# Part of a depthwise convolution handed from VectorE to GpSimd beside attention

## The reference

```python
def conv_group(a, b, conv_w, conv_b, g_ln, b_ln):
    h = a * jax.nn.sigmoid(b)                      # 512 channels
    h = lax.conv_general_dilated(h, conv_w[:, None, :].astype(h.dtype), window_strides=(1,),
                                 padding=[(CONV_K - 1, 0)], dimension_numbers=('NWC', 'WIO', 'NWC'),
                                 feature_group_count=CONV_CH) + conv_b      # CONV_K = 31 taps
    h = layernorm(h, g_ln, b_ln)
    return jax.nn.silu(h)
...
        conv_out = conv_group(z[..., :CONV_CH], z[..., CONV_CH:c0], ...)
        attn_out = mla_group(z[..., c0:c1], z[..., c1:c2], z[..., c2:], pos, ...)   # 8 causal heads
        mixed = jnp.concatenate([rmsnorm(attn_out, g_out_attn[l]), rmsnorm(conv_out, g_out_conv[l])], axis=-1)
        h = h + mixed @ w_out[l]
        h = h + peer_ffn(rmsnorm(h, g_ffn_norm[l]), ...)
```

## Time and profile before

| what | us |
|---|---|
| median of 3 runs | 2993.78 (2993.04 to 2997.05) |
| span of the profiled execution | 2989.1 |
| what lies around the span, as median less span | 4.7 |
| stage `mla` in the trace, first to last instruction | about 125.2 to 263.7 |
| TensorE busy over the span | 2885.6 (97%) |
| DVE, ACT, POOL busy over the span | 1787.5, 999.9, 1035.9 |

### The profile page before, as it was taken

How to read it: one execution, slowest core, us unless ns; L and a number is a source line. 1 busy time by engine, 2 the same in 40 slices (tenths; PEclk the granted TensorE clock), 3 DMA queues, 4 the chain that set the end, 5 groups by cost and what they waited for, 6 DMA issues and landing times. The chain is left out here.

```text
span 2989.1 us, 39368 instructions
## 1 busy us (share of the span) xinstructions
PE 2885.6 (97%) x14960; PEld 2560.3 (86%) x14960; DVE 1787.5 (60%) x3343; ACT 999.9 (33%) x1582; POOL 1035.9 (35%) x642
## 2 busy tenths in 40 slices
PE   8897999999999999999999999999999899899998
PEld 7655799999999999999998887888788788778886
DVE  6776778989888687888885834331043456333211
ACT  4355233444444222222223223222223466322222
POOL 3412400211213242333434444444432344444442
PEclk9997999999999999999999999999999699999999
DMA  3101247787969998999993322233331000222332
GB/s 129 39 1 54 88 146 224 251 271 224 298 205 350 320 330 300 324 325 325 326 325 113 106 85 88 96 99 104 94 133 38 4 1 15 82 95 94 96 102 67
DMA packets 195743, 475.82 MB, mean 159 GB/s; under 512 B 17204, under 2 KB 104116, under 8 KB 193252
## 3 DMA queue, kind: packets, MB, share of 16 engines
q1 hardware_dynamic: 114100, 343.27, 34.5%
q0 software_dynamic: 27648, 100.68, 9.7%
q10 hardware_dynamic: 53808, 29.36, 3.2%
HBM read 415.47 MB, written 56.62 MB: 158 GB/s over the span
## 5 line engine op out<-in xcount | busy, mean ns | idle before, releaser
L263 ACT ACTIVATE w_hi<-w 128x1024 fp32r<-128x1024 f32 (+2 forms) x485 | 506.4, 1046 | 1248.9 <-DVE ffn_gates L2156 324.4
L273 POOL TENSOR_TENSOR w_lo<-w,w_hi 128x1024 fp32r<-128x1024 f32 (+2 forms) x229 | 542.1, 2378 | 697.0 <-ACT w_hi L263 696.9
L273 DVE TENSOR_TENSOR w_lo<-w,w_hi 128x1024 fp32r<-128x1024 f32 x256 | 313.4, 1224 | 149.7 <-ACT w_hi L263 119.1
L308 PE MATMUL peer_psum<-xn_hi,w_hi 128*128 128x416 f32 x1024 | 365.9, 357 | 0.0
L1486 POOL DMA_INDIRECT peer_gathered<-in_peer_u,peer_chosen_here x96 | 152.3, 1586 | 614.0 <-DVEq L1741 483.4
L308 PE MATMUL peer_psum<-peer_w_hi,w_hi 128*128 128x416 f32 x1024 | 359.3, 351 | 3.2 <-DVE peer_w_lo L405 2.4
L309 PE MATMUL peer_psum<-xn_lo,w_hi 128*128 128x416 f32 x1024 | 360.9, 352 | 0.0
L310 PE MATMUL peer_psum<-xn_hi,w_lo 128*128 128x416 f32 x1024 | 360.7, 352 | 0.0
L309 PE MATMUL peer_psum<-peer_w_lo,w_hi 128*128 128x416 f32 x1024 | 358.0, 350 | 0.0
L310 PE MATMUL peer_psum<-peer_w_hi,w_lo 128*128 128x416 f32 x1024 | 358.0, 350 | 0.0
L308 PE MATMUL ffn_psum<-ffn_hn_hi,w_hi 128*128 128x512 f32 x704 | 276.0, 392 | 10.4 <-DVE ffn_hn_lo L618 6.6
(11 more groups left out here) (421 smaller groups left out, 5675.5 us busy)
## 6 DMA issues: line engine op xcount, KB each, us to landing
w<-in_peer_uT SPq DMA_DIRECT2D x128, 512.0 KB, 4.4
w<-in_peer_v SPq DMA_DIRECT2D x128, 512.0 KB, 5.5
w<-in_f_w_gu SPq DMA_DIRECT2D x88, 512.0 KB, 3.6
peer_act<-peer_act_out SPq DMA_DIRECT2D x128, 208.0 KB, 5.4
peer_gate<-peer_gates_out ACTq DMA_DIRECT2D x26, 1024.0 KB, 8.7
peer_gates<-peer_gate SPq DMA_DIRECT2D x16, 1664.0 KB, 9.5
peer_act_in<-peer_act SPq DMA_DIRECT2D x128, 208.0 KB, 4.6
w<-in_f_w_down SPq DMA_DIRECT2D x32, 512.0 KB, 3.5
```

The costliest lines, as they stand in the source:

```text
L263: act.activation(self.hi[:, x, 0:c], self.buf[:, x, 0:c], ACT.Copy).then_inc(self.rounded, 1)
L273: eng.tensor_tensor(self.lo[:, x, 0:c], self.buf[:, x, 0:c], self.hi[:, x, 0:c].bitcast(F32), ALU.subtract).then_inc(self.split, 1)
L308: pe.matmul(out, w[0], x[0], start=start, stop=False)
```

## The change

Three parts of the code change:

- In `front` the 25 taps go to tiles 0 and 1 alone (`POOL_TILE` = 2 caps `there`).
- In `mla` GpSimd makes taps 0 to 21 of tile 2 itself. Tap 0 is one `tensor_scalar` into the accumulator; each other tap is a `tensor_scalar` into one of two slots of a scratch tile (`scale_tap`) and a `tensor_tensor` that adds it to the accumulator (`add_tap`): 22 + 21 instructions of 128x512. They stand in GpSimd's queue between the 31 diagonals: 8 diagonals first, then per tap up to 4/3 further ones ahead of `scale_tap(k+1)` and `add_tap(k)`. The diagonals' `tensor_scalar` gets a second operation (times 1.0).
- VectorE has 93 - 25 - 22 = 46 taps left in `mla`, and `conv_steps` goes from 18 to 16, so `per_step` becomes 3 and all steps that hang on `first` stand two items earlier. A step takes taps of tiles 0 and 1 while there are any (37, so through n = 11 and one more at n = 12); then VectorE waits for all 22 taps of GpSimd (`tap_added`) and goes on with the 9 last taps of tile 2.

TensorE's own code is the same: two taps per item for n up to 15.

```diff
+POOL_TILE, POOL_TAPS = CT - 2, 22
...
-                        conv.run(dve, own, TAPS[key], there)
+                        conv.run(dve, own, TAPS[key], min(there, POOL_TILE))
...
-        conv_steps = 18
+        conv_steps = 16
+        assert conv.taps[on_tensor] == 0 and conv.taps[POOL_TILE] == 0
+        conv.taps[POOL_TILE] = POOL_TAPS
         per_step = -(-(CK * (CT - 1) - sum(conv.taps)) // conv_steps)
-        assert conv.taps[on_tensor] == 0
+        tap_scaled, tap_added = st.sem("tap_scaled"), st.sem("tap_added")
...
             @block.gpsimd
             def _(pool):
-                for k in range(CK):
-                    if k >= DIAGS:
-                        pool.wait_ge(diag_used, k - DIAGS + 1)
-                    pool.tensor_scalar(diag[:, k % DIAGS, :], kit.ident[:, :], kit.gain("conv_w", k * CT + on_tensor), None,
-                                       ALU.mult).then_inc(diag_made, 1)
+                def diagonals(k0, k1):
+                    for k in range(k0, k1):
+                        if k >= DIAGS:
+                            pool.wait_ge(diag_used, k - DIAGS + 1)
+                        pool.tensor_scalar(diag[:, k % DIAGS, :], kit.ident[:, :], kit.gain("conv_w", k * CT + on_tensor), 1.0,
+                                           ALU.mult, ALU.mult).then_inc(diag_made, 1)
+
+                def scale_tap(k):
+                    src = io["conv_in"][:, POOL_TILE, NMETA + k:NMETA + k + SEQ]
+                    w = kit.gain("conv_w", k * CT + POOL_TILE)
+                    if k == 0:
+                        pool.tensor_scalar(acc[:, POOL_TILE, :], src, w, kit.gain("conv_b", POOL_TILE), ALU.mult, ALU.add)\
+                            .then_inc(tap_added, 1)
+                        return
+                    if k >= 3:
+                        pool.wait_ge(tap_added, k - 1)
+                    pool.tensor_scalar(squared4[:, k % 2, :], src, w, 1.0, ALU.mult, ALU.mult).then_inc(tap_scaled, 1)
+
+                def add_tap(k):
+                    pool.wait_ge(tap_scaled, k)
+                    pool.wait_ge(tap_added, k)
+                    pool.tensor_tensor(acc[:, POOL_TILE, :], acc[:, POOL_TILE, :], squared4[:, k % 2, :], ALU.add)\
+                        .then_inc(tap_added, 1)
+
+                made = DIAGS
+                diagonals(0, made)
+                scale_tap(0)
+                scale_tap(1)
+                for k in range(1, POOL_TAPS):
+                    more = min(CK, DIAGS + k * 4 // 3)
+                    diagonals(made, more)
+                    made = more
+                    if k + 1 < POOL_TAPS:
+                        scale_tap(k + 1)
+                    add_tap(k)
+                diagonals(made, CK)
...
                 def between(n):
                     if n < conv_steps:
-                        conv.run(dve, taps, per_step)
+                        own_left = min(per_step, sum(CK - k for k in conv.taps[:POOL_TILE]))
+                        conv.run(dve, taps, own_left, POOL_TILE)
+                        if own_left < per_step and conv.taps[POOL_TILE] < CK:
+                            dve.wait_ge(tap_added, POOL_TAPS)
+                            conv.run(dve, taps, per_step - own_left)
```

## The result

The changed kernel takes 3013.02 us, median of 4 runs (3011.4 to 3013.88), beside 2993.41 us (2990.62 to 2997.05) for the kernel before on the same chip: a ratio of 1.0064 with an interval of 1.005 to 1.0079, slower. The profiled execution took 3012.59 us with a span of 3010.8, so what lies around the span is 1.8 us. For the kernel before it isn't the 4.7 of the prediction either: a further profiled execution of it took 2992.97 us for a span of 2991.0, 2.0 around it, so the execution whose span of 2989.1 the prediction started from was probably one of about 2991 us, quicker than the median.

The account below looks back on a forecast made before the run. TensorE was taken to bound the attention stage, VectorE's taps lying beside its work up to item 15. Terms +14.6 + 5.6 - 1.0 = +19 us on a span of 2989.1 give 3008, plus 4.7 makes 3013; range 2998 to 3025.

Parts of the forecast that it names:

- the 4.7 of the prediction: Around the profiled span: 4.7 us between span and median, added to the span of 3008 to give 3013.
- The new stall: At item 12 in mla, VectorE waits 17.5 us for GpSimd's last add, until 196.8 us, and TensorE's attention work stops.
- even without contention VectorE waits 12 us: At item 12: GpSimd alone is done at 185 us, while VectorE wants its result at 173.2.
- GpSimd's time: GpSimd's queue in mla: 22 scales, 21 adds and 31 diagonals take 58.3 us alone; with contention done at 196.8.
- +0.2 for a diagonal: GpSimd beside VectorE's taps: a diagonal grows by 0.2 us, a scale or an add by 0.45.
- VectorE's pace: VectorE before the wait: 1.15 us a tap beside GpSimd, 4.27 us an item, item 12's tap at 178.3 us.
- The sum for this part: Stage start to carry-over: item 16's carry-over at about 208.7 us against 194.10 for item 18's before, +14.6.
- The 1.5 us for TensorE's low clock: Behind the stall, ahead of the carry-over: TensorE returns with its clock down, which adds 1.5 us.
- second rival: VectorE and GpSimd exclude each other for whole instructions; TensorE also waits for diagonals past item 9: +31 us, 3025; chance 0.12.
- Light contention: GpSimd's long instructions disturb VectorE as little as diagonals do; GpSimd done at 185 us: +7 us, 3001; chance 0.13.
- Not slower: GpSimd is done before VectorE asks at 173.2 us, leaving only the gains of 1.5 and 1 us: 2991; chance 0.05.
- the mis-sized term: Behind the carry-over: two more items cost 5.6 us, and the norms' steps two items earlier give back 1.0.

Follow-up runs that it names:

- The first experiment: Changed kernel, but GpSimd sums its 22 taps in its own tile, joined by one add at the carry-over, so no wait at item 12: 3001.66 us, ratio 1.0041.
- the spare-work run: Kernel before, all 68 VectorE taps kept, with GpSimd doing the changed kernel's 22 taps and 31 diagonals into an unread spare tile: 3014.12 us, ratio 1.0081.
- the two versions with GpSimd's own sum: Changed kernel with GpSimd's 22 taps summed in its own tile and joined at the carry-over: conv_steps 16, 3001.66 us (1.0041); conv_steps 18, 2995.14 us (1.0013).

## Why the prediction was right, and where its terms were off

**The new stall: as said.** VectorE waits once, ahead of tap L667, for GpSimd's add, at item 12: 17.5 us forecast, 16.92 measured; adds at 1.26 us alone and 1.69 beside taps, nine taps behind the wait at 0.77 us (2.31/3), TensorE idle for 11.71 us, its clock at 0.59 behind it. The first experiment confirms the price: without that wait 10.5 of the 19.6 us are gone. What the wait is made of was not as said: "even without contention VectorE waits 12 us" failed, since with no taps beside GpSimd it waits 4.92, and contention makes the larger part of the 16.92.

**GpSimd's time: 3.5 us off, by two errors that partly cancel.** Alone it was put at 58.3 us; it takes 51.9. Adds (26.7 forecast, 26.5 measured) and scales (16.1; 14.5 + 0.8) were right; the diagonal was priced at 0.5 us and takes 0.367, so 4.4 us too much. The old form without the second operation took 0.587 at its quickest; the two-operation row was the better neighbour and still too high. Contention was put at 13 us (196.8 - 125.3 against 58.3) and is 16.2 (68.1 - 51.9), and nearly half of it is on the diagonals: 18.5 - 11.1 = 7.4 us, with 3.9 on the adds and 4.2 on the scales. The step "+0.2 for a diagonal", read off 0.73 against 0.587, failed: a diagonal beside taps goes from 0.36 to 0.80, +0.45 like the long instructions. The price of 0.587 without taps was not the error: in the trace of the kernel before a diagonal of 0.60 us stands at 147.78, between four taps that start at 144.87 and end at 147.60 and the next at 148.47. But the old diagonals overlapped taps only for part of their row, so the mean of 14, 0.73 us, hides what one loses beside a tap: the one at 148.64, beside a tap, took 1.04.

```profile
144.87 2.73 DVE L667 SCALAR_TENSOR_TENSOR mixT<-conv_in,gains,mixT 128x512 f32<-128x512 f32 x4
147.78 0.60 POOL L1164 TENSOR_SCALAR mla_tap_diagonals<-ident,gains 128x128 f32<-128x128 f32 x1 [2.60 <-PE mla_psum L1148]
148.64 1.04 POOL L1164 TENSOR_SCALAR mla_tap_diagonals<-ident,gains 128x128 f32<-128x128 f32 x1 [0.26 <-PE mla_psum L1148]
```

**VectorE's pace.** A tap was put at 1.15 us and an item at 4.27; the 37 taps ahead of the wait take 38.05/37 = 1.03 (busy time of VectorE with line L667 alone, same columns as above but VectorE's only),

```profile
122.20:173.50 51.30, 38.05 (x37) 0.95 0.00 1
```

and an item (172.50 - 124.07)/12 = 4.04. So VectorE reached the wait 51.2 us into the stage, not 54.1, GpSimd was done at 68.1, not 71.6, and the carry-over came at 82.4, not 83.5. The sum for this part was +14.6; it measures +13.5. That is closer than its terms: the wait ends 3.5 us earlier than said, but from there to the carry-over 14.3 us pass and not 11.9. The 1.5 us for TensorE's low clock was too little: VectorE stands 1.75 and 2.54 us for its scores there. The second rival's other part, TensorE waiting for diagonals, did come, in small: twice 1.5 us, at items 10 and 12 (164.03 and 173.72). No cost of it shows, since VectorE's wait ends with GpSimd anyway. Both engines run slower than alone, and neither waits for the whole of the other's instruction each time, which is why the second rival with +31 us did not come. The Trainium skill (SBUF — State Buffer, Who interferes with whom) has the second to issue fully blocked; in the changed kernel's trace that may describe single taps, of which the longest took 1.76 us and the shortest 0.74, but the mean of 1.03 us a tap lies between no contention (0.68) and the 1.48 that the rule gave, and a GpSimd instruction beside taps lost about 0.44 us, less than a tap's 0.68.

**Light contention, not slower.** Light contention is out by the spare-work run: 23 us from contention alone where VectorE has 68 taps. "Not slower" is out by the run with VectorE's taps left out: GpSimd needs 51.9 us by itself and is asked for at 47.0 us in that run, at 51.2 in the changed kernel.

**Behind the carry-over: the mis-sized term.** The prediction had two more items, +5.6, less 1.0 for the norms' steps: +4.6. Measured: +12.0. Two more items are 76.2 - 70.2 = 6.0 us (the norms' steps alone moved back, against all steps moved back), as said. But the norms' earlier place does not gain 1.0, it costs 81.0 - 76.2 = 4.8; another 1.2 (70.2 - 69.0) is little more than the 0.8 by which the two profiles of before differ. The prediction looked at the end of the stage only, at the norm steps behind item 31, and not at TensorE's wait for ScalarE that the silu causes further up (5.19 us before, 6.33 after), nor at the items that stand behind it at the low clock. The stretch from the carry-over to the last copy in the changed kernel and, in the second line, in the one with the norms' steps back (columns of the earlier trace rows) says which of the two costs:

```profile
204.68:285.67 80.99, 66.54 (x267) 40.01 (x267) 35.72 (x74) 47.22 (x109) 2.53 (x2) 0.69 0.00 1
204.27:280.50 76.23, 59.69 (x267) 35.72 (x267) 36.99 (x74) 45.76 (x108) 2.61 (x2) 0.75 0.00 1
```

The same 267 records of products keep TensorE busy for 66.54 us against 59.69, 6.9 more, at a mean granted clock of 0.69 against 0.75, while its idle time is 14.5 us against 16.5, not more. So the 4.8 us are slower work at the low clock, and the waits add nothing in sum.

**And why the time came out at the forecast all the same.** 7.4 us too little in the tail and 1.1 too much ahead of it make the stage 6.3 us longer than forecast. Of this 3.0 are hidden by the earlier start of the stage in the profiled execution, and 0.9 come back behind `peer`'s start, so that the span of 3010.8 is only some 2.5 above the 3008 of the forecast. Around the span the forecast had 4.7 us, and there are 1.8, 2.9 less. The mechanism and the size of the stall are shown; that the median fell on the forecast is luck. The tail's 4.8 us are not equally plain in all times: in the kernel before the earlier steps cost 1.0021 (1.0009 to 1.0032), 4.9 us by the medians, and the two versions with GpSimd's own sum differ by 4.9 as well, but in the changed kernel the two versions that undo the earlier steps, 1.0067 and 1.0061, can't be told from 1.0064. Why is open.

## What to carry to other kernels

Work that is moved to an idle engine is priced twice: by what it takes alone, and by how it slows the engine it relieves; here each VectorE tap beside GpSimd's work grew by half (0.68 to 1.03 us), so a third fewer of them relieved it of next to nothing. A result of the slow engine belongs in a buffer of its own that is joined at the end, where being late costs little, and not in the middle of an ordered queue: that was about 10 of the 19.6 us. And when a constant moves a whole chain of steps, look at each stall that the chain causes and count what stands behind it, not only at its last steps.

## What the hardware showed that was not expected

- A 128x128 `tensor_scalar` on GpSimd with two operations takes 0.36 us alone, the form with one operation and none as the second never less than 0.587 in 31 instances, 0.60 where no tap stands beside it.
- The time that a VectorE tap adds to a GpSimd instruction does not grow with its length: 0.36 to 0.80 us for 128x128, 0.68 to 1.12 for a 128x512 scale, 1.26 to 1.69 for a 128x512 add, about 0.44 each.
- TensorE's granted clock stayed at 0.50, its lower level of 1.2 GHz, from 257.0 to 286.3 us although the engine was busy for 28.16 of 29.30 us. In the earlier trace rows a stretch of 49 us without a gap stands at full clock. In the first profile of the kernel before it came back behind a wait of 5.19 us in time for the last scores (1.35 us at 249.22), behind the 6.33 us here it did not. What kept it down is open.
